# Seven products for a pair of feature tiles in both MLPs' first projections, with the operand sums made on GpSimd

## The reference

```
# first block                                    w_up 1024 x 4096, w_down 4096 x 1024
hn = rms_norm(h, g_mlp_pre)
ff = square(relu(hn @ w_up)) @ w_down
h = h + rms_norm(ff, g_mlp_post)
# second block                                   w_ffn_in 1024 x 5632, w_ffn_out 2816 x 1024
h = rmsnorm(x, ln_ffn_g)
a, u = split(h @ w_ffn_in, 2)                    # 2816 features each
a = causal_dwconv(a, conv_w, conv_b)             # three taps over the tokens
x = x + (silu(a) * u) @ w_ffn_out
```

## Time and profile before

| what | value |
|---|---|
| median of 3 runs | 1450.16 us (1449.21 to 1454.07) |
| profiled execution, span from first to last instruction | 1448.3 us |
| PE, share of the span busy | 99% |
| DVE, ACT, POOL busy | 57%, 39%, 15% |
| mean granted TensorE clock | 0.998 |

### The profile page before, as it was taken

The page is one execution under the profiler, slowest core; times in us unless marked ns, Lnnn a source line. Parts: engine busy times, 40 slices in busy tenths (PEclk is TensorE's granted clock), DMA queues, the critical chain, the costliest instruction groups (busy, mean ns, idle before and its releaser), DMA issues.

```text
span 1448.3 us, 18117 instructions
## 1 busy us (share of the span) xinstructions
PE 1433.9 (99%) x7154; PEld 1188.5 (82%) x7154; DVE 829.5 (57%) x1255; ACT 567.7 (39%) x853; POOL 214.0 (15%) x139
## 2 busy tenths in 40 slices
PE   9999999999999999999999999999999999999998
PEld 6776898888888888887799888888888888888887
DVE  5777488444434346786696736544463755535554
ACT  5345545323223124544464546323241533323320
POOL 4175322000000012430052104000020000000000
PEclk9999999999999999999999999999999999999999
DMA  6222123433323322222211211323332323332332
GB/s 238 88 74 73 59 73 102 115 94 98 102 88 102 102 88 73 88 71 67 82 59 33 71 44 59 116 88 102 98 92 88 102 92 102 98 102 91 99 98 78
DMA packets 36341, 129.86 MB, mean 90 GB/s; under 512 B 4040, under 2 KB 4296, under 8 KB 36256
## 3 DMA queue, kind: packets, MB, share of 16 engines
q1 hardware_dynamic: 35968, 128.44, 28.6%
q10 hardware_dynamic: 288, 0.26, 0.1%
HBM read 126.56 MB, written 2.10 MB: 89 GB/s over the span
## 4 chain that ended last, share of the span: by engine, by line
PE 94%; DVE 3%; ACT 1%; issue 1%; DMA 0%; POOL 0%; SPq 0%; DVEq 0%; POOLq 0%
PE P L1407 24%; PE P L1409 23%; PE P L1408 23%; PE P L1455 3%; PE P L1446 3%; PE P L1448 3%; PE P L1748 1%; PE P L1495 1%; PE P L1496 1%; PE P L1497 1%; PE P L1603 1%; PE P L1704 1%; DVE WL L2170 1%; PE P L1725 1%; PE P L1790 0%
## 5 line engine op out<-in xcount | busy, mean ns | idle before, releaser
L1827 ACT ACTIVATE WH<-WR 128x1024 fp32r<-128x1024 f32 x233 | 245.9, 1056 | 425.2 <-PE P L1409 361.3
L1407 PE MATMUL P<-AH,WH 128*128 128x512 f32 x856 | 342.4, 400 | 0.2 <-DVE BC L2514 0.2
L2170 DVE TENSOR_TENSOR WL<-WR,WH 128x1024 fp32r<-128x1024 f32 x217 | 291.0, 1341 | 78.8 <-ACT WH L1827 78.4
L1409 PE MATMUL P<-AH,WL 128*128 128x512 f32 x856 | 334.4, 391 | 0.0
L1408 PE MATMUL P<-AL,WH 128*128 128x512 f32 x856 | 334.1, 390 | 0.0
L1407 PEld LDWEIGHTS P<-AH,WH 128*128 128x128 f32 x856 | 161.1, 188 | 36.8 <-issue 4.5
L1409 PEld LDWEIGHTS P<-AH,WL 128*128 128x128 f32 x856 | 161.1, 188 | 34.3
L1408 PEld LDWEIGHTS P<-AL,WH 128*128 128x128 f32 x856 | 161.2, 188 | 32.0 <-issue 0.5
L1407 PE MATMUL P<-FH,WH 128*128 128x512 f32 x432 | 168.0, 389 | 0.0
L1408 PE MATMUL P<-FL,WH 128*128 128x512 f32 x432 | 168.0, 389 | 0.0
L1409 PE MATMUL P<-FH,WL 128*128 128x512 f32 x432 | 168.0, 389 | 0.0
(11 more groups left out here) (360 smaller groups left out, 2113.8 us busy)
## 6 DMA issues: line engine op xcount, KB each, us to landing
WR<-in_ws SPq DMA_DIRECT2D x233, 512.0 KB, 3.6
out<-Y SPq DMA_DIRECT2D x8, 256.0 KB, 2.0
H<-in_xT SPq DMA_DIRECT2D x3, 512.0 KB, 8.3
C<-in_const SPq DMA_DIRECT2D x1, 946.5 KB, 11.4
H<-in_xT SPq DMA_DIRECT2D x2, 256.0 KB, 4.2
PR<-in_pT SPq DMA_DIRECT2D x1, 512.0 KB, 4.4
WR<-in_ws SPq DMA_DIRECT2D x1, 384.0 KB, 4.4
GKU<-in_gku SPq DMA_DIRECT2D x1, 160.0 KB, 11.4
```

The source lines that it names most:

```text
L1407: e.matmul(P, wh, xh, start=start, stop=False)
L1409: ins = e.matmul(P, wl, xh, start=False, stop=stop)
L1827: e.activation(m.WH[:, c % NW, :], m.WR[:, c % NRAW, :], ACT.Copy).then_inc(*at.up("w_hi", "w_hi", c))
L2170: e.tensor_tensor(m.WL[:, c % NW, :], m.WR[:, c % NRAW, :], m.WH[:, c % NW, :].bitcast(F32), ALU.subtract).then_inc(*at.up("w_lo", "w_lo", c))
```

## The change

Two feature tiles that share the input (in the first MLP tiles f and f + 1, in the second a and u of one f) are computed as one 2 x 2 block product: rows are the two tiles, the inner dimension is split in even and odd k-tiles, and columns are the two halves of the tokens (256). Seven products of such blocks (each four k-tiles, three matmuls, 256 columns: 12 matmuls) and sums of operands and results replace the eight. It applies to tiles 10 to 31 of the first MLP (11 pairs) and f = 6 to 21 of the second (16 pairs).

For each pair, beside the products:
- GpSimd makes four sums of weight blocks, 128 x 512 each (`s_add` 1 to 4); the weights of a pair become four units (kinds 2, 0, 3, 1) in place of two chunks. ACT copies each to WH; DVE makes WL of kinds 2, 0 and 1, GpSimd that of kind 3, which is half as wide.
- Partial results are copied out of PSUM by ACT (`s_snap`, four of 256 columns) and added by DVE (`s_c11`, `s_c12`) and GpSimd (`s_c22`). A product that accumulates on a bank waits until the snapshot of it is taken.
- The first MLP's relu and square become one DVE instruction that reads SBUF twice (`relu_squared`). In the second MLP GpSimd makes half of `ffn_second`.
Once per MLP four sums of the activations are made and split (`forms`). FH/FL shrink from 16 tiles to 10 (FS), one more raw weight buffer per MLP is found, the bank ring has six banks in these stages, and the plan is aligned to chunks (1872 blocks for 1866).

The core of the diff (the memory map, `Order`'s tables of units and buffers, and `forms` are left out):

```diff
+SLOTS = (1, 5, 6, 2, 7, 3, 4)
+PRODUCT_UNIT = {1: (0, 0), 2: (0, 1), 3: (3, 0), 4: (1, 1), 5: (2, 0), 6: (2, 1), 7: (1, 0)}
+UNIT_ENDS = {6: 2, 2: 0, 3: 3, 4: 1}
...
+    def convert(self, k):
+        self.converted = k
+        if k < len(self.units):
+            self.say("w_hi", k)
+            self.upper.append(k)
+            if k + 1 < len(self.units) and self.units[k + 1][0] == 2:
+                for j in (1, 2, 3):
+                    self.say("s_add", self.units[k + 1][1], j)
 
     def rest(self):
+        for k in self.upper:
+            kind, c = self.units[k]
+            self.say("w_lo_pool" if self.onpool or kind == 3 else "w_lo", k)
+            if kind == 0:
+                self.say("s_add", c, 4)
+            elif kind != 2:
+                self.load(c + 1 if kind == 1 else c)
         self.upper = []
...
+        for slot, k in enumerate(SLOTS):
+            self.tick()
+            if slot == 0:
+                p.x = self.ring()
+            if slot == 1:
+                p.z = self.ring()
+            if slot == 3:
+                p.y = self.ring()
+            for at, what, arg in ((1, "s_snap", 1), (2, "s_snap", 5), (3, "s_snap", 6), (4, "s_c11", None),
+                                  (5, "s_snap", 7), (6, "s_c12", None)):
+                if slot == at:
+                    self.say(what, p, arg)
+            if slot == 4:
+                self.close(p.y)
+            if slot == 6:
+                self.say("s_c22", p)
+                self.close(p.z)
+            if slot in (0, 3, 4, 6):
+                self.convert(self.converted + 1)
+                self.rest()
+            self.say("mm_s", p, k)
+            self.tick()
+        self.beside(post(p))
...
+        def post(p):
+            f = p.f
+            self.say("up_first", p)
+            self.say("up_second", p)
+            self.close(p.x)
+            yield 2
+            self.say("up_split", f)
+            yield 2
+            self.say("up_split", f + 1)
...
+        def post(p):
+            f = p.f
+            self.say("ffn_first", p)
+            yield 2
+            self.say("ffn_taps", f)
+            yield 3
+            self.say("ffn_second", p)
+            self.close(p.x)
+            yield 2
+            self.say("ffn_split", f)
...
+        pairs(range(6, 10))
         down(range(0, 8), 0)
-        pairs(range(16, 22))
+        pairs(range(10, 18))
         down(range(8, 16), 1)
+        pairs(range(18, 22))
         down(range(16, 22), 2)
...
+        if k in (6, 7, 4, 3):
+            w.wait_ge(*at("snap", p.id, {6: 1, 7: 6, 4: 7, 3: 5}[k]))
...
+        for i in range(4):
+            xh, xl = m.form(p.s, k, i)
+            o = 512 * half + 128 * i
+            wh, wl = m.WH[:, u % NW, o:o + 128], m.WL[:, u % NW, o:o + 128]
+            e.matmul(P, wh, xh, start=k in (1, 5, 2) and i == 0, stop=False, skip_group_check=True)
+            e.matmul(P, wh, xl, start=False, stop=False, skip_group_check=True)
+            ins = e.matmul(P, wl, xh, start=False, stop=k in (2, 3, 4) and i == 3, skip_group_check=True)
...
+    def up_second(p):
+        w.wait_ge(*at("s_full", p.id, 4))
+        w.wait_ge(*at("s_c22", p.id))
+        e.activation(m.snap(p, 2), m.bank[p.x.bank][:, cols(0)], ACT.Copy).then_inc(*at.up("snap", "snap", p.id, 4))
...
+    def relu_squared(out, x):
+        return e.scalar_tensor_tensor(out, x, 0.0, x, ALU.max, ALU.mult)
...
+        turn()
+        o, p, q, how = ((s1, a21, a22, ALU.add), (s2, a11, s1, ALU.subtract), (a21, a21, a11, ALU.subtract),
+                        (a12, a12, s2, ALU.add))[j - 1]
+        e.tensor_tensor(o, p, q, how).then_inc(*at.up("s_add", "s_add", c, j))
...
+    def s_c22(p):
+        x = m.snap(p, 3)
+        w.wait_ge(*at("snap", p.id, 7))
+        turn()
+        e.tensor_tensor(x, x, m.snap(p, 2), ALU.add).then_inc(*at.up("s_c22", "s_c22", p.id))
```

More of the change, by code:

```diff
@@ L203, in ring @@
     def ring(self):
-        i = min((j for j in range(4) if not self.open[j]), key=lambda j: self.closed[j])
+        i = min((j for j in self.banks if not self.open[j]), key=lambda j: self.closed[j])
         self.open[i] = True
@@ L254, in tile, with pair, forms @@
         return t
+    def pair(self, s, first, second, f, post):
+        c = len(self.plan) // CH
+        assert len(self.plan) % CH == 0
+        self.found.append((c, s))
+        for spec in (first, second):
+            for half in (0, 1):
+                self.plan.extend(spec[j] for j in range(half, 8, 2))
+        p = Pair(self.npairs, s, c, self.pair_units.get(c), f)
+        self.npairs += 1
+        p.before = self.in_stage.get(s, [None, None])[-2]
+        self.in_stage.setdefault(s, [None, None]).append(p)
+        for slot, k in enumerate(SLOTS):
[17 more added lines that the diff above has]
+                self.convert(self.converted + 1)
+                self.rest()
+            self.say("mm_s", p, k)
+            self.tick()
+        self.beside(post(p))
+    def forms(self, s):
+        self.say("t_diff", s)
+        yield 4
+        self.say("t_u", s)
+        yield 3
+        self.say("t_2", s)
+        yield 3
+        self.say("t_3", s)
+        yield 3
+        self.say("t_4", s)
+        yield 3
+        for j in (1, 2, 3):
+            self.say("t_split", s, j)
+            yield 3
     def narrow(self, name, c0, n, kind):
@@ L745, in mlp1, with pairs @@
         self.paced(*(lambda f=f: up(f, out[f]) for f in range(7)))
-        up(7, self.tile(fu(7), A))
+        for f in range(7, 10):
+            t = self.tile(fu(f), A)
+            up(f, t)
+        self.last_plain["2"] = t
+        self.beside(self.forms("2"))
+        def post(p):
[7 more added lines that the diff above has]
+            self.say("up_split", f + 1)
+        def pairs(fs):
+            for f in fs[::2]:
+                self.pair("2", fu(f), fu(f + 1), f, post)
         def down(g):
@@ L755, in down @@
                     self.say("square", "p2", m, 1)
[L756 to L759, removed]
+        down(0)
+        self.finish()
+        self.banks = (0, 1, 2, 3, 6, 7)
+        self.say("t_split", "2", 4)
+        self.align()
+        pairs(range(10, 18))
+        down(1)
+        pairs(range(18, 26))
+        down(2)
+        pairs(range(26, 32))
+        self.banks = (0, 1, 2, 3)
         down(3)
@@ L1384, in weights @@
     def weights(i, n=1):
[L1386 to L1387 removed]
+        k, o = order.unit_of[i // CH], (i % CH) * 128
+        if k == 0:
             w.wait_ge(*at("w_hi0", int(o >= FIRST)))
@@ new lines, in s_c22, with t_diff @@
+    def s_c22(p):
[3 more added lines that the diff above has]
+        e.tensor_tensor(x, x, m.snap(p, 2), ALU.add).then_inc(*at.up("s_c22", "s_c22", p.id))
+        did("s_c22", p.id)
+    def t_diff(s):
+        for i in range(0, 8, 2):
+            for b in range(2):
+                w.wait_ge(*at("h", s, i, b))
+        x = m.H[:, :, :].rearrange("p (i q) t -> p i q t", q=2)[:, :, 0, :]
+        turn()
+        e.tensor_tensor(m.t_raw(s, 1), x[:, :, cols(1)], x[:, :, cols(0)], ALU.subtract).then_inc(
+            *at.up("t_diff", "t_diff", s))
+        did("t_diff", s)
@@ L2841, in square, with ffn_second @@
+    def ffn_second(p):
+        f, b = p.f, cols(1)
+        w.wait_ge(*at("s_c22", p.id))
+        w.wait_ge(*at("ffn_silu", f))
+        w.wait_ge(*at("x_lo", "F2", f - 2))
+        turn()
+        e.tensor_tensor(m.GG4[:, f % 2, b], m.snap(p, 3), m.SS4[:, f % 4, b], ALU.mult).then_inc(
+            *at.up("ffn_u2", "ffn_u2", f))
+        at.also(("ffn_u2", f), "sn_free", p.id)
+        did("ffn_u2", f)
     def square(n, i, direct, a=None):
```

439 lines of the change are left out of this document (356 added, 83 removed).

## The result

The changed kernel takes 1552.28 us, the median of four runs (1551.88 to 1552.99); the kernel before took 1450.81 us beside it. The ratio is 1.0699, with an interval of 1.0684 to 1.0714: 7% slower. The forecast was 1543 us in a range of 1475 to 1580.

A forecast was written before the change was run, and what follows sets the result against it. TensorE's matmul time was taken as the bound (busy 99% of the span). Span 1448.3 + 66 (second MLP) + 11 (first MLP) + 4 (head and last `down`) + 12 (clock) = 1541, plus 1.9 to the median: 1543 us, range 1475 to 1580.

The forecast's parts named there:

- The saving on TensorE: All 27 pairs: matmul time falls from 10.85 to 10.08 us a pair, 20.8 us in all.
- the edge of the last `down`: End of the second MLP: the last `down` needs f = 21 soon after its last product, +2 us.
- Turns between DVE and POOL: Pairs: two-input DVE operations and POOL additions alternate, 11.8 to 12.4 us a pair; first MLP +11 us.
- The prediction's check of the turns: Profile before, from 222.5 us: 6.17 us read as DVE and POOL instructions run one after another.
- The queue order in the second MLP: Product 6 waits for snapshot 1 behind `w_lo`, taps and silu; stand 6 us, with turns +66 us.
- The undisturbed stand: Second MLP, before product 6: without POOL interference the product is still 2.3 us late.
- the clock +12: Second MLP: stands lower the granted clock in 8 of 13 pairs, 1.5 us of slow matmuls each, +12 us.
- third rival: Clock falls in every pair and cold matmuls also delay unit copies: 1560 to 1585 us, chance 0.09.
- The head: Start of the second MLP's pairs: snapshot 1 waits for the last activation split, 0 to 4 us, taken +2.
- The sign of being wrong "product 1 waiting for `w_lo` of kind 0": Pairs: a TensorE gap there would mean POOL's chain, not the silu, is the bound; no size given.
- The first rival: Pairs: queues delay, turns do not; 1464 us, chance 0.24 together with a partial meeting at some 1480.
- the second (TensorE never waits): All pairs fit under TensorE: 1429 us, chance 0.06 including a stall short enough to turn the sign.

The follow-up runs named there:

- e2: Changed kernel with GpSimd's four weight sums cut to 8 columns after the first pair of each MLP: 1496.41 us.
- e7: Changed kernel with e1's snapshot order, the second MLP's first `down` ahead of its pairs, most pairs alone between `down` tiles: 1467.77 us.
- e4: Changed kernel with each GpSimd weight sum replaced by two constant fills of the same size, which read nothing: 1507.91 us.
- e1: Changed kernel with each of a pair's four snapshots named one step earlier on ACT's queue: 1509.73 us.
- e3: Changed kernel with the edits of e1 and e2 together: 1462.54 us.
- e5: Changed kernel with 20 or 32 unused 256-column matmuls before product 6 in the second MLP's waiting pairs: 1537.34 us.
- e10: e7 with the second MLP's split three steps later, `down` halves moved near both ends, and a last-tiles addition on POOL: 1467.1 us.

## Why the prediction was right

**The saving on TensorE** (20.8 us) is there: where nothing holds it up a pair takes 10.07 to 10.08 us (e2, e7), 84 matmuls at 0.120. It was priced correctly and swallowed: the pairs of both MLPs, 21 us below the plain tiles in matmul time, came out 87 us above them, with the edge of the last `down`.

**Turns between DVE and POOL** were right as a mechanism. e4 separates them from POOL being busy: the same occupation without reading leaves the taps at 0.75 us. In the first MLP they are the whole loss (e2: from 12.75 us a settled pair to 10.08, while e1 changes nothing). The term was +11 and measured +6. Most of that, 3.4 us, is the last pair of each run: it has no weight sums behind it and took 12.0 us, where the sum put 13.1. The settled pair took 12.75, the second 11.35 against 11.4. The prediction's check of the turns (three times 1.18, 0.56, twice 1.07) adds up to 6.24 us and not to the 6.17 read; the rows above bear the three holds out all the same.

**The queue order in the second MLP** was right: the chain `w_lo`, taps, silu, snapshot 1 is the row-by-row reading above, and e1 takes 42 us out by moving snapshot 1. The prediction did not look past product 6: snapshot 6, for product 7, hangs on the same silu (e1, e3). The stand was forecast as 6 us and is 4.6 to 4.9, in the last pair of a run 2.7 to 2.8; with the clock held up it is 5.7 (e5). The undisturbed stand was forecast as 2.3 and is up to 2.5 (e2). Turns and queue together were +66, the clock +12, the edge of the last `down` +2, in sum +80; measured +81, of which about 15 are the clock (e5).

**That these terms meet so closely is in part luck.** The clock falls in all thirteen pairs that wait for the silu, not in eight, and costs 1.9 us of slow matmuls in a settled pair, not 1.5. The forecast's +12 comes near the 15 because slow matmuls also shorten the next stand, which it did not foresee. Half of the third rival's condition came true (the clock falls in every pair); its time did not.

**The head** is the mis-sized term: "0 to 4, I take +2" became +15. The work was counted correctly but set against the wrong cover. Timeline of DVE there, and TensorE's stand:

```profile
1155.69 1.67 DVE L2534 SCALAR_TENSOR_TENSOR TW<-H,PM,SN 128x256 f32<-128x256 f32 x4
1157.27 1.67 DVE L2541 SCALAR_TENSOR_TENSOR SN<-H,PM,TW 128x256 f32<-128x256 f32 x4
...
1161.83 1.67 DVE L2552 SCALAR_TENSOR_TENSOR TL<-TW,PM,TH 128x256 fp32r<-128x256 f32 x4 [1.69 <-ACT TH L2138]
...
1164.56 2.35 DVE L2557 TENSOR_TENSOR TL<-TW,TH 128x1024 fp32r<-128x1024 f32 x2
1166.83 0.68 DVE L3165 TENSOR_TENSOR AP<-P,RBC 128x512 f32<-128x512 f32 x1
1168.39 0.75 DVE L3181 SCALAR_TENSOR_TENSOR SS<-AP,PM,SS 128x512 f32<-128x512 f32 x1 [0.88 <-ACT SS L2460]
1169.18 0.75 DVE L3184 SCALAR_TENSOR_TENSOR SS<-AP,PM,SS 128x512 f32<-128x512 f32 x1
1169.85 1.22 DVE L2507 TENSOR_TENSOR WL<-WX,WH 128x1024 fp32r<-128x1024 f32 x1
```

```profile
1171.17 0.55 PE L1665 MATMUL P<-AH,WH 128*128 128x256 f32 x1 [13.62 <-issue]
```

Not product 6 waits here but the first matmul of the first pair. Its weights' low part (1169.85) stands on DVE's queue behind the sums and nearly all splits of the activations, and behind the scaling and the two taps of the last plain tile (3.0 us of it). DVE does most of that work from 1155.7 on instead of beside the four tiles before. The prediction asked when the last split was due, not what stands behind it.

**The edge of the last `down`** was +2 and is 3.9 in one wait (third row of the waits above) and 1.9 of slow matmuls behind it.

In all the terms miss by -5 (first MLP), +13 (head) and +1 (pairs of the second MLP with that edge), which makes 102 of the 93 forecast. The +1 is again a balance: +6 for that edge was +2, and the pairs alone are +75 where +78 was forecast. The sign of being wrong "product 1 waiting for `w_lo` of kind 0" shows in the first MLP alone (0.6 us, five times), where no silu is in the chain and the forecast's own cycle ends with that `w_lo`. The first rival (turns don't matter) falls by e2 and by the alternating rows, the second (TensorE never waits) by the first row of waits.

**What stays open.** In e7 to e10 the pairs that stand alone in the second MLP mostly keep 0.9 to 1.5 us each. The rows show the silu waiting for taps, and the taps start late; that this comes from POOL's last sum, through ACT's copy of kind 3, was read off the timeline and not isolated. What makes the first pairs of the second MLP stand for longer in e10 was not followed, nor whether the reading or the arithmetic of POOL's additions is what holds DVE up. No version with pairs in the second MLP came out below plain tiles there.

## What to carry to other kernels

When work is taken from a saturated engine and given to others, price it by what the others do at the same time: two engines that each have room may have none together, if they take turns, as VectorE and GpSimd did here. Then look at the queue of each engine for what stands ahead of the result that the saturated engine wants next, the first such result above all, where a batch of preparation is still ahead of it. When one such result is moved out of the way, look for the next one behind the same instruction (e1). Give such a stage other matmuls in between (here 10.9 us of `down` after each pair) before adding engines to it.

## What the runs showed of the hardware that was not expected

- GpSimd fills (`memset`, 128 x 512, 0.53 us) that ran without a pause left VectorE's operations with two operands at their undisturbed 0.74 and 0.75 us; GpSimd additions beside them made those 1.63 and 1.75. e4's theory had this; the prices are the runs'.
- TensorE stood still from 1291.2 us on. Its granted clock was at 0.50 from 1294, stayed there when work began again at 1296.06, and was back at 1.00 at 1301. Stands of 4.6 to 4.9 us were each followed by some 1.9 us lost to slow matmuls. Matmuls that nobody needs, put into the stand, kept the clock at 1.00 and made the kernel 15 us faster.
- The length of a stand alone does not tell what the clock does behind it. In e1 three stands of 3.35 us, ending at 1313.89, 1341.75 and 1448.14, were followed by a mean granted clock of 0.72, 0.50 and 1.00 in the next 5 us. In e2 a stand of 1.92 us, ending at 1413.50, was followed by 0.50 from 1415 to 1418.
